# Small modulation products sent through column tiles in a two-layer diffusion backbone on one core

## The reference

```
silu_c, silu_cc = silu(c), silu(c_ctx)          # two vectors of 1024
for l in range(2):
    mod   = silu_c  @ w_mod[l] + b_mod[l]       # w_mod[l] is 1024 x 6144
    mod_c = silu_cc @ w_mod[l][:, :n] + b_mod[l][:n]
    ... shift, scale, gate = slices of mod (latent) and mod_c (context)
```

## Time and profile before

| | |
|---|---|
| median of 3 runs | 5231.02 us (5228.61 to 5240.66) |
| the profiled execution, its own time | 5233.87 us |
| its span | 5232.0 us |
| mean granted TensorE clock | 0.835 of full |
| PE busy | 70% of the span |
| DVE busy | 63% |
| GpSimd busy | 43% |
| ACT busy | 28% |
| mean DMA rate | 300 GB/s |

### The profile page before, as it was taken

How to read it: one execution, slowest core, us unless ns; L and a number is a source line. 1 busy time by engine, 2 the same in 40 slices (tenths; PEclk the granted TensorE clock), 3 DMA queues, 4 the chain that set the end, 5 groups by cost and what they waited for, 6 DMA issues and landing times. The chain is left out here.

```text
span 5232.0 us, 49044 instructions
## 1 busy us (share of the span) xinstructions
PE 3682.9 (70%) x15944; PEld 1874.4 (36%) x15944; DVE 3285.6 (63%) x6632; ACT 1478.5 (28%) x3634; POOL 2236.0 (43%) x1698
## 2 busy tenths in 40 slices
PE   7988888886878875555555557978987555555555
PEld 5576424322277421111111126877843111111111
DVE  5164676664365466777767757657355767677775
ACT  2152334342042222222222223244212222222221
POOL 3153434443033245555555543333314555555554
PEclk8888999998988987777777778988999777777777
DMA  5435999998602599999999972201259999999998
GB/s 181 161 101 186 395 373 405 396 420 359 232 1 102 223 380 417 414 408 415 405 415 409 408 314 73 73 17 73 81 197 353 419 403 411 416 403 417 411 413 360
DMA packets 248128, 1574.52 MB, mean 301 GB/s; under 512 B 41776, under 2 KB 45360, under 8 KB 61616
## 3 DMA queue, kind: packets, MB, share of 16 engines
q0 software_dynamic: 184320, 1342.26, 62.8%
q1 hardware_dynamic: 63552, 229.13, 12.2%
HBM read 1555.39 MB, written 15.89 MB: 300 GB/s over the span
## 5 line engine op out<-in xcount | busy, mean ns | idle before, releaser
L2199 PE MATMUL banks<-arena 128*64 128x512 f32 x5120 | 1648.8, 784 | 1217.6 <-ACT arena L2052 1216.8
L1850 POOL DMA_INDIRECT arena<-in_experts,arena x1280 | 1483.1, 1159 | 1683.1 <-PE banks L2199 1432.7
L1938 DVE CUSTOM_DVE_ANT_0 arena<-arena,token_copies 128x1024 f32<-128x1024 f32 x1280 | 1644.3, 1302 | 734.9 <-DMA arena<-in_experts,arena 677.8
L2199 PEld LDWEIGHTS banks<-arena 128*64 128x64 f32 x5120 | 397.9, 171 | 2326.0 <-ACT arena L2052 1678.3
L2045 ACT ACTIVATE arena<-arena 128x2 f32<-128x2 f32 x640 | 131.2, 205 | 1878.5 <-DVE arena L1938 1874.9
L278 POOL TENSOR_TENSOR wide_low<-wide_blocks,wide_high 128x1024 fp32r<-128x1024 f32 x152 | 381.7, 2532 | 603.3 <-ACT wide_high L268 603.3
L2052 ACT ACTIVATE arena<-arena 128x64 f32<-128x64 f32 x1280 | 375.9, 340 | 287.8 <-POOL arena L1737 245.9
L316 PE MATMUL banks<-activation_a,wide_high 128*128 128x256 f32 (+1 forms) x896 | 318.3, 355 | 9.5 <-ACT arena L340 2.7
L318 PE MATMUL banks<-activation_a,wide_low 128*128 128x256 f32 (+1 forms) x896 | 308.4, 344 | 0.0
L2100 PE MATMUL banks<-arena,wide_blocks 128*128 128x512 f32 (+1 forms) x768 | 296.7, 532 | 2.5 <-ACT arena L1969 2.5
L2153 PE MATMUL banks<-arena,wide_blocks 128*128 128x512 f32 x576 | 279.3, 623 | 0.0
(11 more groups left out here) (236 smaller groups left out, 5022.3 us busy)
## 6 DMA issues: line engine op xcount, KB each, us to landing
wide_blocks<-in_wide SPq DMA_DIRECT2D x170, 1024.0 KB, 4.8
arena<-in_experts,arena POOLq DMA_INDIRECT x1280, 10.8
pre_scan<-arena SPq DMA_DIRECT2D x16, 256.0 KB, 7.3
arena<-pre_scan SPq DMA_DIRECT2D x16, 256.0 KB, 5.3
residual<-in_tokens SPq DMA_DIRECT2D x6, 512.0 KB, 8.1
arena<-mod_rows SPq DMA_DIRECT2D x6, 512.0 KB, 7.0
norm_rows<-in_keys SPq DMA_DIRECT2D x3, 1024.0 KB, 6.0
pre_z<-arena SPq DMA_DIRECT2D x8, 256.0 KB, 7.4
```

The source lines that it names most:

```text
L1850: pool.indirect_dma_start(out=v.ring[:, g % RING], out_offset=None, in_=io["experts"], in_offset=bass.IndirectOffsetOnAxis(ap=c.idx[:, u % ...
L1938: last = nc.vector.tensor_tensor_reduce(out=u_row, in0=u_row, in1=k.copies[:, n % NJ], scale=1.0, scalar=0.0, op0=ALU.mult, op1=ALU.add, a ...
L2199: mm = nc.tensor.matmul(k.ps[j * QUAD:(j + 1) * QUAD, a + half], v.lhs[:, g % 4, j], v.ring[:, (g * NJ + j) % RING, D + half * BANK:D + (h ...
```

## The change

The 8 products of a block in `more_mods` now use a stationary operand of 32 columns (the two vectors and 30 columns of zeros) and go to four column tiles: slice `kt` writes to partitions `32q` to `32q+31` with `q = kt % 4`, so that each quadrant accumulates two products. ACT copies the whole 128 x 256 to a buffer `parts`; then a new matmul with a stationary operand `pick` (128 x 2, ones in rows 0 and 1 of each quadrant) sums the four quadrants into `ps[0:2, 6 + i % 2, 256:512]`, the bias product is added to that, and ACT copies the two rows as before. The summing of block i-1 (`combine`) is placed behind the products of block i. Block i waits until the rows of block i-2 have been copied, as before.

```diff
 def multiply(pe, i):
-    n = w0 + i
-    pe.wait_ge(wide_landed of block n)
-    if i % per == 0:
-        pe.wait_ge(k.mod_bias.sem, bias0 + 16 * (i // per + 1))
-    if i >= 2:
-        pe.wait_ge(k.mod_used.sem, used0 + i - 1)
-    out = k.ps[0:2, 6 + i % 2, 0:WIDE]
-    for kt in range(KT):
-        signal_used(k, nc.tensor.matmul(out, k.csil[:, kt], k.wide[:, n % WIDE_SLOTS, kt], start=(kt == 0), stop=False))
-    nc.tensor.matmul(out, k.ones[0:1, 0:2], rows[...], start=False, stop=True).then_inc(k.mod_ready.sem, 1)
-    k.used_up += 1
+    if i < count:
+        n = w0 + i
+        pe.wait_ge(wide_landed of block n)
+        if i >= 2:
+            pe.wait_ge(k.mod_used.sem, used0 + i - 1)
+        for kt in range(KT):
+            q = kt % 4
+            last = nc.tensor.matmul(k.ps[32 * q:32 * q + 32, 6 + i % 2, 0:WIDE], k.csil[:, kt],
+                                    k.wide[:, n % WIDE_SLOTS, kt], start=(kt < 4), stop=(kt >= 4))
+            signal_used(k, last)
+        last.then_inc(k.mod_parts.sem, 1)
+        k.used_up += 1
+    if i >= 1:
+        combine(pe, i - 1)
+
+def combine(pe, i):
+    if i % per == 0:
+        pe.wait_ge(k.mod_bias.sem, bias0 + 16 * (i // per + 1))
+    pe.wait_ge(k.mod_moved.sem, moved0 + i + 1)
+    out = k.ps[0:2, 6 + i % 2, WIDE:2 * WIDE]
+    nc.tensor.matmul(out, k.pick[:], parts[:, i % 2], start=True, stop=False)
+    nc.tensor.matmul(out, k.ones[0:1, 0:2], rows[...], start=False, stop=True).then_inc(k.mod_ready.sem, 1)

 def take(act, i):
-    act.wait_ge(k.mod_ready.sem, ready0 + i + 1)
-    nc.scalar.copy(rows[...], k.ps[0:2, 6 + i % 2, 0:WIDE]).then_inc(k.mod_used.sem, 1)
+    if i < count:
+        act.wait_ge(k.mod_parts.sem, parts0 + i + 1)
+        if i >= 2:
+            act.wait_ge(k.mod_ready.sem, ready0 + i - 1)
+        nc.scalar.copy(parts[:, i % 2], k.ps[:, 6 + i % 2, 0:WIDE]).then_inc(k.mod_moved.sem, 1)
+    if i >= 1:
+        last = i - 1
+        act.wait_ge(k.mod_ready.sem, ready0 + last + 1)
+        nc.scalar.copy(rows[...], k.ps[0:2, 6 + last % 2, WIDE:2 * WIDE]).then_inc(k.mod_used.sem, 1)
```

More of the change, by code:

```diff
@@ L382, in _ @@
             act.wait_ge(k.cols_loaded.sem, 16)
-            nc.scalar.activation(k.csil[:], cvec, ACT.Silu).then_inc(k.h_ready.sem, 1)
+            act.wait_ge(k.consts_set.sem, 1)
+            nc.scalar.activation(k.csil[:, :, 0:2], cvec, ACT.Silu).then_inc(k.h_ready.sem, 1)
         @block.gpsimd
@@ L398, in _ @@
                 for kt in range(KT):
-                    last = nc.tensor.matmul(k.ps[0:2, n % 2, 0:WIDE], k.csil[:, kt], k.wide[:, slot, kt],
+                    last = nc.tensor.matmul(k.ps[0:2, n % 2, 0:WIDE], k.csil[:, kt, 0:2], k.wide[:, slot, kt],
                                             start=(kt == 0), stop=(kt == KT - 1))
@@ L422, in stage_mods, with more_mods @@
     return n_blk
-def more_mods(k, layer, first, rows, w0, rounds, per):
+def more_mods(k, layer, first, rows, parts, w0, rounds, per):
     nc, io = k.nc, k.io
     ready0, used0, bias0, kept0 = k.mod_ready.base, k.mod_used.base, k.mod_bias.base, k.mod_kept.base
-    span = per * WIDE
+    parts0, moved0 = k.mod_parts.base, k.mod_moved.base
+    parts = parts.rearrange("p (a c) -> p a c", a=2)
+    span, count = per * WIDE, rounds * per
     def load(sp, r):
@@ L465, in done @@
+        if i >= 1:
+            last = i - 1
+            act.wait_ge(k.mod_ready.sem, ready0 + last + 1)
+            nc.scalar.copy(rows[0:2, (last % per) * WIDE:(last % per + 1) * WIDE], k.ps[0:2, 6 + last % 2, WIDE:2 * WIDE]) \
+                .then_inc(k.mod_used.sem, 1)
     def done(sp):
         sp.wait_ge(k.mod_kept.sem, kept0 + 16 * rounds)
-    count = rounds * per
     m = Bag()
     m.load, m.keep, m.multiply, m.take, m.done, m.count = load, keep, multiply, take, done, count
-    for x in (k.mod_ready, k.mod_used):
+    for x in (k.mod_ready, k.mod_used, k.mod_parts, k.mod_moved):
@@ L678, in stage_states @@
              if ctx or o < NT - 1]
-    mods = more_mods(k, 0, 8, k.gates[:].rearrange("p a c -> p (a c)"), w0, 1, 16) if w0 is not None else None
+    mods = more_mods(k, 0, 8, k.gates[:].rearrange("p a c -> p (a c)"), v.scr[:, 3 * D:3 * D + 512], w0, 1, 16) if w0 is not None else None
     with nc.Block() as block:
@@ L751, in _ @@
             nc.scalar.activation(v.ctot[:, nt], v.cum[:, nt, 32:64], ACT.Exp).then_inc(k.dt_act.sem, 1)
-            for i in range(mods.count if mods else 0):
+            for i in range(mods.count + 1 if mods else 0):
                 mods.take(act, i)
@@ L775, in _ @@
                 last.then_inc(k.state_ready.sem, 1)
-                for i in range(2 + 2 * n, 4 + 2 * n if n < len(steps) - 1 else mods.count) if mods else ():
+                for i in range(2 + 3 * n, 5 + 3 * n if n < len(steps) - 1 else mods.count + 1) if mods else ():
                     mods.multiply(pe, i)
@@ L1352, in _ @@
             for g in range(4):
-                for i in range(7 * g, min(7 * g + 7, mods.count)):
+                for i in range(7 * g, min(7 * g + 7, mods.count + 1)):
                     mods.multiply(pe, i)
@@ L1368, in _ @@
                 nc.scalar.copy(dst, k.ps[:, m % 4].rearrange("p (t c) -> p t c", c=P)).then_inc(k.turn_copied.sem, 1)
-            for i in range(mods.count):
+            for i in range(mods.count + 1):
                 mods.take(act, i)
@@ L2315 @@
         "tri": np.stack([tri, tri.T], axis=1),
+        "pick": np.tile(np.eye(32, 2, dtype=np.float32), (4, 1)),
         "fold": np.tile(np.eye(QUAD, dtype=np.float32), (NJ, 1)),
```

28 lines of the change are left out of this document (15 added, 13 removed).

## The result

The changed kernel takes 5152.82 us (median of six runs, 5148.94 to 5163.03) where the kernel before takes 5237.56 us (median of six, 5228.61 to 5240.66). The ratio is 0.9844 [0.9831, 0.9857]: faster by 1.56%, 82 us of 5237.6 (75 to 88). The forecast was 5179 us with a range of 5162 to 5212.

The account below looks back on a forecast made before the run. PE alone was taken to end both stretches of the 40 blocks. Gains of 24 us (`stage_states`) and 28 (reload stage), together 52, took the profiled 5233.87 to 5182, which stands 2.9 above the median: 5179 us, range 5162 to 5212.

Parts of the forecast that it names:

- What bounds the two stretches: Stretches of the 40 `more_mods` blocks: PE alone ends both; it is busy 74.26 of 74.30 and 37.07 of 37.10 us.
- Four tiles at once: A block's products in `more_mods`: four matmuls run side by side, 0.88 us, and 1.01 until the next matmul starts.
- the switch: Entering and leaving the column tiles on PE: about 0.1 to 0.15 us, taken as 0.13.
- Rival B: Products in `more_mods`: only two tiles overlap, 1.9 us a block, 28 us of gain lost, about 5207 us; chance 0.14.
- the 1.1 that the prediction worked out: A block's products if each tile is worth 0.79: four give 3.2x, about 1.1 us in place of 0.88.
- The step of 2.70: Time from block to block in both stretches: 2.70 us, range 2.5 to 3.0.
- a third limit near by: Weight loads through the slots: two steps take at least 5.4 us, so one at least 2.70.
- `stage_states`, 24: Blocks of `stage_states`: the last copy ends at 220.8 where it was 244.86, a gain of 24 us.
- The reload stage, 28: Blocks of the reload stage: a gain of 37 us, less 9 charged for low clock after three stands, 28.
- Rival C: Both stretches: the clock stays low, steps grow to about 4.57 us, the kernel is slower at 5244 us; chance 0.05.
- The step that failed: Clearing, one small constant load and the shorter constants load, beside much longer transfers: 0 to 0.5 us.

Follow-up runs that it names:

- e2: The changed kernel with the `pick` buffer laid out behind the arena, which then starts at byte 93664; 5198.38 us, 0.9912 of the kernel before.
- e6: The changed kernel with a block's slot freed by the picking matmul instead of the next block's first product; 5149.05 us, 0.9837 of the kernel before.
- e7: The changed kernel with two more wide loads issued ahead of each round's stores and next bias load; 5158.96 us, 0.9853 of the kernel before.
- e8: The changed kernel with 34 spare matmuls filling PE's stands in the reload stage; 5151.52 us, 0.9835 of the kernel before.
- e10: The changed kernel with all three bias rows loaded at the reload stage's start and wide loads issued ahead of the stores; 5135.7 us, 0.9809 of the kernel before.
- e5: The changed kernel with slices dealt to the column tiles as q = kt // 2 instead of kt % 4; 5155.11 us, 0.9838 of the kernel before.
- e1: The changed kernel's buffer sizes and places with the old two-column products; 5204.83 us, 0.9926 of the kernel before.
- e4: The kernel before with 224 unused bytes ahead of the arena, which then starts at byte 92928; 0.9924 of the kernel before.
- e12: As e11, with three small constants laid out first so residual, wide blocks and token copies start at multiples of 256; 5124.63 us, 0.9791 of the kernel before.
- e11: The changed kernel with bias rows loaded at the reload stage's start, wide loads ahead of stores, slots freed by the picking matmul; 5122.11 us, 0.9793 of before.
- e3: The kernel before with 32 unused bytes ahead of the arena, which then starts at byte 92736; 0.9976 of the kernel before.
- e9: The kernel before with 96 unused bytes ahead of the arena, which then starts at byte 92800; 0.9978 of the kernel before.

## Why the prediction was wrong, point by point

**What bounds the two stretches: right.** PE's products did. With products and pick at 84.0 us of busy time in place of 153.7, the two stages lose 40.7 us in the profile, or 46 (39 to 53) by e2 in the times.

**Four tiles at once: right.** The term was 0.88 for the products and 0.13 for entering the tiles, 1.01; the pick starts 0.86 to 0.89 behind the first product, and four sets of 0.215 are 0.86, so the switch costs 0.03 at most. Rival B (two at a time) would have shown 1.9, and the 1.1 that the prediction worked out beside its term is not borne out either. The prediction read 0.1 to 0.15 for the switch out of the earlier trace rows, but 1.86 less 1.78 is 0.08.

**The step of 2.70: right, a little high.** It is 2.52 to 2.55 where nothing waits for a load, mostly since the switches cost so little, and 2.69 on average with the slot's waits, which were forecast as a third limit near by. e6 shows both apart.

**`stage_states`, 24: 19.5 in this profile, about right over the executions.** From the first product (168.69) to the end of the last rows copy (223.63) it takes 54.9 us, where some 50 were forecast. Two dips of the clock, which the sum did not charge in this stage, lie in the windows at 181.00 (0.55) and 218.40 (0.57), both behind a wait for a slow load (1.71 and 1.92 us). These dips belong to the single execution. e7 and e8, whose code for this stage is the changed kernel's, had none before the last blocks and took 61.2 and 61.6 us for the stage, 25 less than the 86.90 before; e10 took 67.6. The sum is inside what the executions show, 19 to 26.

**The reload stage, 28: too large, 21.2 in the profile** (15 in that of e5, whose tiles take the slices in another order). Each stand was found where it was put. Block 3 starts 34.9 us behind the stage's start, where 32.3 was worked out (1317.3 - 1285.0): its load needs 8.1 us, from 1294.66, not 5.7. The interval over the first round's end is 7.97 us (block 9 at 1325.93, block 10 at 1333.90) and 8.52 over the second (block 17 at 1361.57), where 7.6 was forecast. The low clock cost about 12 and not 9: six steps of 4.0 to 4.25 in place of 2.53 are 10, and two steps partly in it, before block 7 and before block 19, add 2.5. And one more wait stood before block 16, 3.50 us at 1358.24, for a load that was slow for a reason that stays open (the same step of 5.47 us took 4.62, 5.63 and 4.87 in e2, e5 and e7, but 2.81 in e8). The last rows copy ends at 1389.2, where 1375 was the forecast with a shift of 24 from the first stage, of which 17 came (the stage begins at 1267.84, before at 1285.03).

**Rival C, the low clock: a part, not a case.** PE pauses 0.54 us in each block and is busy 23.98 of 30.70 us, at 0.99. Once full, the clock is at its lower level only behind the stands: for some 11 of the 54.9 us of `stage_states`, about the two short windows, and for some 58 us in the reload stage, where the low clock reaches over several blocks each time. A step at the lower level takes 4.22, not the 4.57 of this rival.

**The step that failed** is the one that priced the rest of the edit: "the clearing by GpSimd, one small constant load [...] and the shorter constants load lie in stages where they stand beside much longer transfers; 0 to 0.5 us". The sum counted what these edits issue. It took no account of what the buffers that grew do to the addresses of all that is laid out behind them. The arena moved from 32 bytes past a multiple of 256 to a multiple of 256, and gave 0.74% [0.61, 0.88], 39 us, in e1, and 0.76% in e4 by a shift alone. With the arena held off (e2) the kernel runs at 0.9912 of before, 5185 us of the 5231 from which the prediction was made: 6 above the forecast and inside its range. The products gave 46 us (39 to 53) where the sum had 52, and the profiles put what is missing in the reload stage. The range was too narrow because that term was set to zero at both ends. It was luck that the term helped here. The same move the other way would, by the same 39 us, have hidden most of the gain of the products.

Not all of the layout's effect is accounted for by the packets. The mean falls by 2.6 ns in e1 and e4, 27 us by the same working, and the times fall by 39 and 40 (32 to 47). The rest may lie in the other transfers or in what the gathers hold up; no run separates them. The 8 KB packets of the hardware queues are shorter in the changed kernel, 353.5 ns in the mean for 358.0, but not through the arena's place: they are at 360.6 in e1 and in e4. And e12, which aligned the wide blocks as well, gained nothing (350.9 after 351.0 in e11). The intervals of e3 and e9 (0.24 and 0.22% faster) don't reach 1, but e3's packets are no shorter in the mean, so what gives them stays open. That the shorter packets cause the gain of e4 is thus argued from their time and number; that the arena's place causes it is shown.

## What to carry to other kernels

A diff that changes the size of any buffer in front of a large one moves the target of all its DMAs: add up the offsets before and after, and price the move whenever a stage runs with its DMA engines full. To tell such an effect from the edit itself, give the old kernel the new layout, or a few unused bytes; two such runs (e1, e4) settled what no reading of the changed lines could. And when the products of a stage are made faster, read next what frees the buffers and in what order one queue issues loads and stores: here such edits (e11) brought the ratio from 0.9844 to 0.9793.

## What was not expected of the hardware

Of the 8 KB packets of the gathers 95 to 96% take 309 ns when the buffer that they go to starts at a multiple of 256 bytes, and 31% when it starts 32 bytes past one, most of the others 313 or 320; in a kernel whose stages with such gathers take about 3650 us, the move was worth 0.7%. Four column tiles of 32 columns ran four matmuls side by side with no loss (16 records of 256 float32 columns in 0.86 to 0.89 us against 3.54 before), and going into the tiles and out of them cost 0.03 us at most, where the earlier trace rows give 0.08.
